# The adaLN modulation of a decoder step computed from fp32 weights as the stationary operand

## Chip, cores and metric

One NeuronCore of a Trainium2 chip. The metric is the device time of one execution in microseconds, the median of several runs. Everything (prompt group and sample group, both layers) runs in one launch on this core.

## The reference

One inference step of a decoder with two layers, for 512 prompt tokens and 8 sample tokens (one for each of 8 sequences), width 1024. A layer is three sub-layers: a SwiGLU feed-forward part (width 2816), a token mixer, another feed-forward part. That makes six sub-layers, numbered 0 to 5; 1 is the attention and retention mixer ("even"), 4 the convolution mixer ("odd"). Each sub-layer needs a shift, a scale and a gate of 1024 values for each of nine conditioning vectors (one for the prompt, eight for the samples), and it is these that the change concerns:

```python
mods = (jax.nn.silu(c) @ w_ada[l] + b_ada[l]).reshape(B, 1, N_MOD, D_MODEL)
sh, sc, g = mods[:, :, 0], mods[:, :, 1], mods[:, :, 2]
f = _swiglu(x * (1.0 + sc) + sh, w_ffn_in[l, 0], w_ffn_out[l, 0])
x = _layernorm(DEEPNORM_ALPHA * x + 0.5 * g * f, ln_g[l, 0], ln_b[l, 0])
```

`c` has 1 + 8 rows of 1024, `w_ada[l]` is 1024 x 9216 in fp32, so one sub-layer's share is 1024 x 3072, 24 column tiles of 128 (`MT`). Both groups share every weight.

## The kernel before

The activations lie turned in SBUF: 128 partitions of features, 8 tiles (`KT`), the 520 tokens in two halves of 260 (`HT`). SyncE loads the raw weights in chunks of 128 output columns (`raw`, two buffers), ScalarE makes the high part (`cut`, line 1204), POOL the low part (line 656), both two buffers deep, and TensorE multiplies (`product`). A sub-layer's first product runs over its input matrix. The second product makes 8 output tiles: in a feed-forward part two chunks of 11 tiles for each (66 matmuls a chunk), in a mixer one chunk of 8 tiles (48 matmuls). VectorE adds each output tile to the residual (`residual`) and gathers the sums for the norm; `shift_sums` and `norm_sums` (lines 802 to 819) are TensorE's part in that.

The modulation of sub-layer 0 is made at the start, from `ada_first` with the conditioning vectors stationary, plain fp32, and turned afterwards. That of sub-layers 1 to 5 is made during the second product of the sub-layer before, so in the stages of sub-layers 0 to 4, and there the change lies. Before, it goes in 24 pieces a stage. A piece is one half (4 of the 8 row tiles) of 256 columns of the weights, 512 KB, in one of `NADA` = 3 buffers (`ada_w`, line 169). Its way:

- SyncE loads it (`pieces`, line 456), once the low part of the piece three back has been cut. The table `PIECES` (line 50) says which pieces go with which chunk of the product: for a feed-forward tile 0 and 1, then 2, then 3 and 4, then 5; for a mixer three with each chunk. SyncE's queue holds chunk loads and piece loads in that order.
- ScalarE makes its high part (`high_piece`, line 1376). POOL makes the low part in feed-forward stages, VectorE in mixer stages (`low_pieces`, line 425).
- TensorE multiplies (`pieces`, lines 728 and 730): the conditioning vectors are stationary as 18 columns (9 high, 9 low, `c_parts`) with the high part of the weights moving, then as 9 columns with the low part moving, 256 columns at a time, 8 matmuls a piece. The result is 18 x 256 in PSUM.
- After two pieces ScalarE copies that to SBUF (`group_sums`, line 1381) and TensorE turns it and adds the rows of high and low (`turn_group`, line 715): two fp32 matmuls of 18 x 128 by 9 columns, into PSUM bank 6. 12 groups a stage (`GROUPS`), the last turned behind the last product.

TensorE's order is written by hand: in a feed-forward product the first piece of the chunk stands in the middle (after 30 matmuls) and a second one behind the product; in a mixer product pieces stand after 18 and 36 of the 48 matmuls and behind it. VectorE reads bank 6 in `modulation(n)` (line 1499) between the residuals and the norm.

Line 894 (`tri` or `ones`, 128 x 128 fp32, stationary, 8 columns moving) and line 912 (`kr_tok`, 128 x 128 fp32, 128 columns moving) are other fp32 matmuls of the even mixer, line 802 the sums at mid-stage.

Of the kernel before, what the change touches and what calls it, by code (L numbers as in the profile page):

```python
# [22 lines left out]
KT = D // 128  # L23
# [9 lines left out]
MT = 3 * KT  # L33
# [12 lines left out]
NADA = 3  # L46
ADA_W = 256
GROUPS = MT * 128 // ADA_W

# [20 lines left out]
def host_tables():  # L70
# [22 lines left out]
    for m in range(4):  # L93
# [6 lines left out]
    two_parts = np.zeros((128, 9), f)  # L100
    two_parts[np.arange(18), np.arange(18) % 9] = 1
    res = np.concatenate([ident, ones, ones / D, p[:, None].astype(f), gdec, tail.reshape(128, 32),
                          delta.reshape(128, 64), sel.reshape(128, 1024), bd, unit.reshape(128, 64), two_parts], axis=1)
# [20 lines left out]
def build_step(nc, a, out, last=NSUB):  # L124
# [10 lines left out]
    with ctx:  # L135
# [18 lines left out]
        def sem(name):  # L154
# [13 lines left out]
        ada_w = put("ada_w", [128, NADA, KT // 2, ADA_W], F32, R_ADA)  # L168
        ada_sums = put("ada_sums", [18, ADA_W], F32, R_ADA + NADA * 4096)

        ada_parts = {place: tuple(put(f"ada_{part}_{name}", [128, NADA, KT // 2, ADA_W], F32R, at + u * NADA * 4096)
                                  for u, part in enumerate(("hi", "lo")))
                     for place, name, at in ((False, "h", R_H), (True, "proj", R_HID))}
# [21 lines left out]
        res = new("res", [128, 1710])  # L196
# [6 lines left out]
        two_parts = res[0:18, 1701:1710]  # L203
# [4 lines left out]
        c_parts = new("c_parts", [128, KT, 18], F32R)  # L208
# [129 lines left out]
        ada_hi_cut = sem("ada_hi_cut")  # L338
        ada_cut = sem("ada_cut")
        ada_turned = sem("ada_turned")  # L340
# [78 lines left out]
        def low_pieces(eng, n, i, now):  # L419

            hi, lo = ada_parts[n == EVEN]
            for q in now:
                eng.wait_ge(ada_hi_cut, n * MT + i * 6 + q + 1)
                eng.tensor_tensor(lo[:, q % NADA], ada_w[:, q % NADA], hi[:, q % NADA].bitcast(F32),  # L425
                                  ALU.subtract).then_inc(ada_cut, 1)

# [21 lines left out]
        def _(sp):  # L449
# [1512 lines left out]
```

## Time and profile before

| | |
|---|---|
| median of 3 runs | 2734.92 us (2734.47 to 2747.84) |
| profiled execution, span from first to last instruction | 2743.9 us |
| PE busy / weight loads busy | 2498.2 us (91%) / 2240.8 us (82%) |
| VectorE / ScalarE / POOL busy | 918.1 / 846.3 / 1084.8 us |
| granted TensorE clock, mean | 0.940 |
| DMA | 298.44 MB, mean 109 GB/s |

The runs' times don't say which of them was profiled; the span is all that the profile has of its own execution, and it lies within the three runs. PE is TensorE's matmuls, PEld its weight loads, which overlap them. Each row of a timeline is a start, a length, and a line of the kernel; matmuls are pipelined, so the distance of two starts says what one occupies, not its length. The clock is a share of 2.4 GHz: 1.00 is 2.4, 0.50 is 1.2.

### The profile page before, as it was taken

How to read it: one execution, taken by the hardware profiler on the slowest of the kernel's cores; microseconds unless marked ns; L12 is line 12 of the kernel's file. 1: busy time of each engine (PE TensorE's matmuls, PEld its weight loads, DVE VectorE, ACT ScalarE, POOL GpSimd, SP SyncE). 2: the span in 40 equal slices, each digit the busy share in tenths (PEclk: the TensorE clock that was granted, in tenths of full speed). 3: DMA queues.
4: the chain of work that ended last, by engine and by line, in shares of the span. 5: the costliest groups of instructions: out<-in, count | busy, mean ns of one | idle time of the engine just before them, and what ended most of it. 6: DMA issues, size and time to landing. Idle time of an engine off the chain costs nothing.

```text
span 2743.9 us, 45520 instructions
## 1 busy us (share of the span) xinstructions
PE 2498.2 (91%) x18440; PEld 2240.8 (82%) x18440; DVE 918.1 (33%) x1069; ACT 846.3 (31%) x1176; POOL 1084.8 (40%) x544
## 2 busy tenths in 40 slices
PE   7999999799889988699999889999979886999996
PEld 2899999679742347599999889999969875999995
DVE  1122202446244445622211442220253456222214
ACT  3222333422212233332232342233333243322213
POOL 1344476424300011344466644447643323444343
PEclk9999999889969988899999989999989997999998
DMA  7233454247313334233355323335412351333321
GB/s 262 63 91 92 124 158 141 75 131 221 102 59 98 114 94 151 65 89 92 92 156 158 94 62 92 92 116 166 141 39 85 101 175 56 96 89 90 94 87 51
DMA packets 448322, 298.44 MB, mean 109 GB/s; under 512 B 20103, under 2 KB 422119, under 8 KB 448087
## 3 DMA queue, kind: packets, MB, share of 16 engines
q1 hardware_dynamic: 448214, 296.92, 36.3%
q8 instruction: 78, 1.28, 0.2%
q14 instruction: 30, 0.24, 0.0%
HBM read 291.36 MB, written 5.53 MB: 108 GB/s over the span
## 4 chain that ended last, share of the span: by engine, by line
PE 57%; DVE 7%; issue 3%; DMA 2%; ACT 2%; POOL 2%; SPq 0%; DVEq 0%; POOLq 0%; ACTq 0%
PE ps L706 45%; PE ps L975 2%; PE ps L728 1%; PE ps L730 1%; PE ps L961 1%; PE ps L965 1%; DMA raw<-w_out_odd 1%; DMA raw<-w_out_even 1%; DVE sq_sum L1588 1%; DVE ada_lo_proj L425 1%; PE ps L1014 1%; DVE ada_lo_h L425 1%; PE ps L1007 1%; DVE rdev L1626 1%; POOL w_lo L656 1%
## 5 line engine op out<-in xcount | busy, mean ns | idle before, releaser
L656 POOL TENSOR_TENSOR w_lo<-raw,w_hi 128x1024 fp32r<-128x1024 f32 (+1 forms) x308 | 802.6, 2607 | 1255.4 <-ACT w_hi L1204 1254.9
L706 PE MATMUL ps<-h_hi,w_hi 128*128 128x260 f32 x3584 | 730.0, 285 | 25.3 <-POOL w_lo L656 15.9
L706 PE MATMUL ps<-h_hi,w_lo 128*128 128x260 f32 x3584 | 728.5, 285 | 0.0
L706 PE MATMUL ps<-h_lo,w_hi 128*128 128x260 f32 x3584 | 728.3, 285 | 0.0
L1204 ACT ACTIVATE w_hi<-raw 128x1024 fp32r<-128x1024 f32 (+1 forms) x308 | 346.6, 1126 | 1233.4 <-PE ps L706 1121.3
L706 PEld LDWEIGHTS ps<-h_hi,w_hi 128*128 128x128 f32 x3584 | 560.0, 191 | 30.4 <-POOL w_lo L656 13.2
L706 PEld LDWEIGHTS ps<-h_hi,w_lo 128*128 128x128 f32 x3584 | 559.6, 191 | 0.0
L706 PEld LDWEIGHTS ps<-h_lo,w_hi 128*128 128x128 f32 x3584 | 558.7, 191 | 0.0
L706 PE MATMUL ps<-hid_hi,w_hi 128*128 128x260 f32 x1408 | 286.6, 285 | 13.8 <-DVE hid_lo L1920 13.8
L706 PE MATMUL ps<-hid_hi,w_lo 128*128 128x260 f32 x1408 | 284.9, 284 | 0.0
L706 PE MATMUL ps<-hid_lo,w_hi 128*128 128x260 f32 x1408 | 284.2, 284 | 0.0
L1917 DVE TENSOR_TENSOR gated<-silu_a,ps 128x520 f32<-128x520 f32 x88 | 61.3, 696 | 663.2 <-PE ps L706 647.2
L706 PEld LDWEIGHTS ps<-hid_hi,w_hi 128*128 128x128 f32 x1408 | 219.0, 190 | 16.7 <-DVE hid_lo L1920 14.7
L1558 DVE SCALAR_TENSOR_TENSOR x<-ps,mod,x 128x512 f32<-128x512 f32 x48 | 36.1, 751 | 567.6 <-PE ps L706 567.6
L1920 DVE TENSOR_TENSOR hid_lo<-gated,hid_hi 128x520 f32 (+1 forms) x88 | 196.9, 2238 | 81.9 <-ACT hid_hi L1475 81.9
L706 PEld LDWEIGHTS ps<-hid_lo,w_hi 128*128 128x128 f32 x1408 | 219.2, 190 | 0.0
L706 PEld LDWEIGHTS ps<-hid_hi,w_lo 128*128 128x128 f32 x1408 | 218.3, 190 | 0.0
L425 POOL TENSOR_TENSOR ada_lo_h<-ada_w,ada_hi_h 128x1024 fp32r<-128x1024 f32 x72 | 171.3, 2393 | 46.3 <-ACT ada_hi_h L1376 46.3
L746 PE MATMUL ps<-h_hi,w_hi 128*128 128x260 f32 x192 | 48.9, 341 | 85.2 <-DVE h_lo L1549 85.1
L746 PEld LDWEIGHTS ps<-h_hi,w_hi 128*128 128x128 f32 x192 | 34.5, 222 | 99.2 <-issue 88.8
L728 PE MATMUL ps<-ada_hi_h,c_parts 128*18 128x256 f32 x384 | 96.0, 284 | 12.6 <-DVE ada_lo_h L425 12.6
L1376 ACT ACTIVATE ada_hi_h<-ada_w 128x1024 fp32r<-128x1024 f32 x96 | 97.5, 1044 | 20.3 <-DMA ada_w<-w_ada 17.1
(296 smaller groups left out, 2375.8 us busy)
## 6 DMA issues: line engine op xcount, KB each, us to landing
raw<-w_ffn_in SPq DMA_DIRECT2D x176, 512.0 KB, 3.7
ada_w<-w_ada SPq DMA_DIRECT2D x120, 512.0 KB, 4.4
raw<-w_ffn_out SPq DMA_DIRECT2D x64, 704.0 KB, 4.4
pages<-cache_k SPq DMA_DIRECT2D x64, 256.0 KB, 3.0
pages<-cache_v SPq DMA_DIRECT2D x64, 256.0 KB, 3.0
raw<-w_in_even SPq DMA_DIRECT2D x28, 512.0 KB, 4.1
raw<-w_in_odd SPq DMA_DIRECT2D x24, 512.0 KB, 3.7
ada_first<-w_ada SPq DMA_DIRECT2D x5, 2048.0 KB, 14.3
```

Source lines behind the costliest of these rows:

```text
L425: eng.tensor_tensor(lo[:, q % NADA], ada_w[:, q % NADA], hi[:, q % NADA].bitcast(F32), ALU.subtract).then_inc(ada_cut, 1)
L656: pool.tensor_tensor(w_lo[:, k, 0:kt, :], raw[:, k, 0:kt, :], w_hi[:, k, 0:kt, :].bitcast(F32), ALU.subtract).then_inc(chunk_cut, 1)
L706: mm = pe.matmul(ps[:, 2 * q + half, 0:HT], w[:, k, t, :], v[:, kt0 + t, half, :], start=start and t == 0 and step == 0, stop=stop and t = ...
L728: pe.matmul(ps[0:18, 7, 0:ADA_W], c_parts[:, at, :], hi[:, q % NADA, t, :], start=at == 0, stop=False)
L730: mm = pe.matmul(ps[0:9, 7, 0:ADA_W], c_parts[:, at, 0:9], lo[:, q % NADA, t, :], start=False, stop=at == KT - 1)
L746: mm = pe.matmul(ps[:, 2 * q + half, 0:HT], w[:, k, t, :], v[:, t, half, :], start=t == 0 and step == 0, stop=t == KT - 1 and step == 2)
L975: mm = pe.matmul(ps[0:NH, 7, :], s_samp[:, b, :, g], pages[:, k, g % 4, :], start=g == 0, stop=g == NPG - 1)
L1204: act.activation(w_hi[:, k, 0:kt, :], raw[:, k, 0:kt, :], ACT.Identity).then_inc(hi_cut, 1)
L1376: act.activation(hi[:, q % NADA], ada_w[:, q % NADA], ACT.Identity).then_inc(ada_hi_cut, 1)
L1558: dve.scalar_tensor_tensor(xt[:, :, 0:HP], ps[:, 2 * q:2 * q + 2, 0:HP], g[:, 0:1], xt[:, :, 0:HP], ALU.mult, ALU.add).then_inc(drained, 1)
L1917: dve.tensor_tensor(gated[:, j], silu_a[:, j], pair(2 * j + 1), ALU.mult).then_inc(gate_done, 1)
L1920: dve.tensor_tensor(hid_lo[:, m].rearrange("p a h c -> p (a h) c"), gated[:, j], hid_hi[:, m].rearrange("p a h c -> p (a h) c").bitcast(F3 ...
```

## The change

A piece is now one column tile of 128 with all 8 row tiles, again 512 KB, as plain fp32 in one of 4 buffers. TensorE takes the weights themselves as the stationary side (128 x 128) and moves the nine conditioning vectors (`c_act`, fp32), 8 matmuls a piece, straight into the 9 columns of bank 6 that belong to the tile. There are still 24 pieces a stage at the same places. SyncE loads a piece once TensorE has used the one four back. The high and low parts of the pieces, `c_parts`, the copies, the turning, and their semaphores go. The bodies of second products on SyncE and TensorE are written out in full, 4 times. The modulation of sub-layer 0 stays.

```diff
-NADA = 3
-ADA_W = 256
-GROUPS = MT * 128 // ADA_W
+NADA = 4
...
-        ada_w = put("ada_w", [128, NADA, KT // 2, ADA_W], F32, R_ADA)
+        ada_w = put("ada_w", [128, NADA, KT, 128], F32, R_ADA)
...
-                    if not (n == 1 and is_first(i) and q < NADA):
-                        sp.wait_ge(ada_cut, c - NADA + 1)
-                    half = q % 2 * (KT // 2)
-                    sp.dma_start(ada_w[:, q % NADA, :, :],
-                                 ada_view(n)[:, half:half + KT // 2, bass.ds(i * 3 * ADA_W + q // 2 * ADA_W, ADA_W)]
-                                 ).then_inc(ada_full[q % NADA], 16)
+                    if c >= NADA:
+                        sp.wait_ge(ada_used, MT + c - NADA + 1)
+                    at = (i * 6 + q) * 128
+                    sp.dma_start(ada_w[:, c % NADA, :, :], ada_view(n)[:, :, at:at + 128]).then_inc(ada_full[c % NADA], 16)
...
-                    if q % 2 == 0 and not (is_first(i) and q == 0):
-                        turn_group(n, i * 3 + (q // 2 - 1))
-                    pe.wait_ge(ada_cut, (n - 1) * MT + i * 6 + q + 1)
-                    for t in range(KT // 2):
-                        at = q % 2 * (KT // 2) + t
-                        pe.matmul(ps[0:18, 7, 0:ADA_W], c_parts[:, at, :], hi[:, q % NADA, t, :],
-                                  start=at == 0, stop=False)
-                        mm = pe.matmul(ps[0:9, 7, 0:ADA_W], c_parts[:, at, 0:9], lo[:, q % NADA, t, :],
-                                       start=False, stop=at == KT - 1)
+                    c, tile = (n - 1) * MT + i * 6 + q, i * 6 + q
+                    if tile == 0:
+                        pe.wait_ge(mod_steps, mod_steps_before(n))
+                    pe.wait_ge(ada_full[c % NADA], c // NADA * 16 + 16)
+                    for t in range(KT):
+                        mm = pe.matmul(ps[:, 6, tile * 9:tile * 9 + 9], ada_w[:, c % NADA, t, :], c_act[:, t, :],
+                                       start=t == 0, stop=t == KT - 1)
                     mm.then_inc(ada_used, 1)
...
-                if n + 1 < last:
-                    turn_group(n + 1, GROUPS - 1)
+                for i in range(KT // 2):
+                    body(i)
...
-                        if n + 1 == last and chunk:
+                        if chunk:
                             cut(*chunk)
-                        if n + 1 < last:
-                            then = (steps + (tuple(q + 6 for q in steps[0]),))[u + 1]
-                            if static and i == KT // 2 - 1 and then[0] >= 6:
-                                then = ()
-                            modulation_parts(i, now, then, chunk)
...
-                    dve.wait_ge(ada_turned, GROUPS * n)
+                    dve.wait_ge(ada_used, MT * (n + 1))
...
-                        if n not in FFN and n + 1 < last:
-                            low_pieces(dve, n, i, PIECES[1][j])
```

## Rows read from the trace of the kernel before

**Rows 1.** the page: shares of the chain that ended last
```profile
PE 57%; DVE 7%; issue 3%; DMA 2%; ACT 2%; POOL 2%; SPq 0%; DVEq 0%; POOLq 0%; ACTq 0%
PE ps L706 45%; PE ps L975 2%; PE ps L728 1%; PE ps L730 1%; PE ps L961 1%; PE ps L965 1%; DMA raw<-w_out_odd 1%; DMA raw<-w_out_even 1%; DVE sq_sum L1588 1%; DVE ada_lo_proj L425 1%; PE ps L1014 1%; DVE ada_lo_h L425 1%; PE ps L1007 1%; DVE rdev L1626 1%; POOL w_lo L656 1%
```
**Rows 2.** stretches: busy PE, PEld, DVE, ACT, POOL; clock; sub-layers 1, 4, 0, 2, 5
```profile
1013.80:1123.50 109.70, 90.39 (x629) 81.18 (x629) 59.11 (x69) 41.40 (x53) 18.46 (x8) 0.85 0.47 144
2189.40:2293.80 104.40, 86.14 (x629) 77.91 (x629) 58.08 (x69) 40.69 (x53) 17.78 (x8) 0.90 0.51 152
336.60:496.50 159.90, 158.69 (x1297) 152.14 (x1297) 28.07 (x40) 50.98 (x59) 108.25 (x40) 0.99 0.48 139
1405.80:1564.40 158.60, 157.34 (x1297) 150.82 (x1297) 28.10 (x40) 51.00 (x59) 108.30 (x40) 1.00 0.47 140
2578.50:2708.10 129.60, 129.56 (x1060) 129.24 (x1060) 28.11 (x40) 24.27 (x22) 46.12 (x14) 0.99 0.25 73
```
**Rows 3.** who waited for whom in 1013.8 to 1123.5: total, times, longest
```profile
ACT ada_hi_proj L1376 <- DMA ada_w<-w_ada: 19.8, 8, 6.7
...
PE ps L728 <- DVE ada_lo_proj L425: 13.8, 4, 5.2
```
**Rows 4.** timeline of PE, even mixer stage: start us, us, what
```profile
1056.80 0.40 PE L706 MATMUL ps<-h_hi,w_lo 128*128 128x260 f32 x2
1057.13 0.61 PE L715 MATMUL ps<-res,ada_sums 18*128 18x9 f32 x4
1057.67 0.29 PE L728 MATMUL ps<-ada_hi_proj,c_parts 128*18 128x256 f32 x1
...
1058.61 0.40 PE L706 MATMUL ps<-h_hi,w_hi 128*128 128x260 f32 x2
```
**Rows 5.** groups of instructions, the turning
```profile
L715 PE MATMUL ps<-res,ada_sums 18*128 18x9 f32 x240 | 36.9, 259 | 14.8 <-ACT ada_sums L1381 14.8
```
**Rows 6.** timeline of PE, two runs of fp32 matmuls
```profile
747.29 0.57 PE L894 MATMUL ps<-logf,even_t 128*128 128x8 f32 x2 [2.67 <-DVE rot L1692]
...
751.13 0.57 PE L894 MATMUL ps<-logf,even_t 128*128 128x8 f32 x2
...
764.72 3.50 PE L912 MATMUL ps<-vr_tok,kr_tok 128*128 128x128 f32 x29 [3.27 <-DVE kr_tok L1717]
```
**Rows 7.** stretches, same columns, at the two runs of group 6
```profile
747.00:752.00 5.00, 4.71 (x21) 4.45 (x22) 4.59 (x7) 0.00 (x0) 0.00 (x0) 0.50 0.00 2
764.70:768.00 3.30, 3.28 (x29) 3.28 (x30) 0.00 (x0) 0.00 (x0) 0.00 (x0) 1.00 0.76 251
```
**Rows 8.** timeline of PE, a change from products to fp32 and back
```profile
425.09 0.40 PE L706 MATMUL ps<-hid_hi,w_lo 128*128 128x260 f32 x2
425.33 1.04 PE L802 MATMUL ps<-tile_sum,res 128*128 128x260 f32 x4
...
426.32 0.28 PE L730 MATMUL ps<-ada_lo_h,c_parts 128*9 128x256 f32 x1
```
**Rows 9.** timeline of PE, start of the odd mixer's second product
```profile
2189.38 0.80 PE L706 MATMUL ps<-mix_hi,w_hi 128*128 128x260 f32 x2 [0.77 <-DVE mix_lo L1890]
...
2193.34 0.28 PE L728 MATMUL ps<-ada_hi_h,c_parts 128*18 128x256 f32 x1
```
**Rows 10.** DMA issues: KB each, median us to landing
```profile
ada_w<-w_ada SPq DMA_DIRECT2D x120, 512.0 KB, 4.4
...
raw<-w_out_even SPq DMA_DIRECT2D x8, 512.0 KB, 5.7
```
**Rows 11.** the page: groups that cut a chunk of weights
```profile
L656 POOL TENSOR_TENSOR w_lo<-raw,w_hi 128x1024 fp32r<-128x1024 f32 (+1 forms) x308 | 802.6, 2607 | 1255.4 <-ACT w_hi L1204 1254.9
...
L1204 ACT ACTIVATE w_hi<-raw 128x1024 fp32r<-128x1024 f32 (+1 forms) x308 | 346.6, 1126 | 1233.4 <-PE ps L706 1121.3
```
**Rows 12.** timeline of PE, end of the even mixer's second product
```profile
1121.10 0.40 PE L706 MATMUL ps<-h_hi,w_lo 128*128 128x260 f32 x2
...
1126.12 1.14 PE L816 MATMUL ps<-sq_sum,res 128*128 128x260 f32 x4 [0.65 <-DVE sq_sum L1588]
```

More of the change, by code:

```diff
@@ L167, in build_step @@
         R_ADA = region(4 * 4096)
-        ada_w = put("ada_w", [128, NADA, KT // 2, ADA_W], F32, R_ADA)
[L169 to L174, printed above, removed]
+        ada_w = put("ada_w", [128, NADA, KT, 128], F32, R_ADA)
         R_TMP = region(5 * 4 * NTOK)
@@ L194, in build_step @@
         dev = sq[:, 0]
-        res = new("res", [128, 1710])
+        res = new("res", [128, 1701])
         ident, ones, mean_w = res[:, 0:128], res[:, 128:256], res[:, 256:384]
@@ L207, in build_step @@
         c_act = new("c_act", [128, KT, 9])
-        c_parts = new("c_parts", [128, KT, 18], F32R)
         mod = new("mod", [128, 2, MT, 9])
@@ L417, in centre_tile @@
             eng.tensor_tensor(x[:, t], x[:, t], mean[:, :, :], ALU.subtract).then_inc(centred[part], 1)
[L419 to L426, printed above, removed]
         two = lambda v: v.rearrange("p (h c) -> p h c", h=2)
@@ L590, in _ @@
                         sp.wait_ge(rows_made, 6)
-                    loop(sp, n == 0, KT // 2, body)
+                    for i in range(KT // 2):
+                        body(i)
                     continue
@@ L611, in body @@
                             pieces(n + 1, i, PIECES[1][k])
-                loop(sp, False, KT // 2, body)
+                for i in range(KT // 2):
+                    body(i)
                 if n == ODD:
@@ L679, in second_body @@
                                 cut(c, u % 2, kt)
-                                if n in FFN and n + 1 < last:
-                                    low_pieces(pool, n, i, now)
                         loop(pool, False, KT // 2, second_body)
@@ L1079, in second_product @@
             def second_product(n, body):
-                loop(pe, True, KT // 4, body)
-                body(KT // 4)
-                body(KT // 4 + 1)
-                if n + 1 < last:
-                    turn_group(n + 1, GROUPS - 1)
+                for i in range(KT // 2):
+                    body(i)
             for n in range(last):
@@ L1368, in second_product @@
                 steps = PIECES[per_tile]
-                hi = ada_parts[n == EVEN][0]
-                def high_piece(i, q):
-                    if not (is_first(i) and q < NADA):
-                        act.wait_ge(ada_used, (n + 1) * MT + i * 6 + q - NADA + 1)
-                    act.wait_ge(ada_full[q % NADA], n * MT // NADA * 16 + i * 32 + q // NADA * 16 + 16)
-                    act.activation(hi[:, q % NADA], ada_w[:, q % NADA], ACT.Identity).then_inc(ada_hi_cut, 1)
-                def group_sums(i, q):
-                    act.wait_ge(ada_used, (n + 1) * MT + i * 6 + q + 1)
-                    act.activation(ada_sums[:, :], ps[0:18, 7, 0:ADA_W], ACT.Identity).then_inc(rows_copied, 1)
-                def modulation_parts(i, now, then, chunk=None):
-                    cuts = [((now[-1] if len(now) > 1 else now[-1] + 1) - 0.5, 2, 0)] if chunk else []
-                    for _, what, q in sorted([(q, 0, q) for q in now if q % 2] + [(q - NADA, 1, q) for q in then] + cuts):
-                        if what == 2:
-                            cut(*chunk)
-                        elif what == 0:
-                            group_sums(i, q)
-                        elif q < 6:
-                            high_piece(i, q)
-                        else:
-                            high_piece(i + 1, q - 6)
                 def body(i):
@@ L1423, in second_product @@
                     act.wait_ge(ev("cat_lo"), 10)
-                if n + 1 < last:
-                    modulation_parts(0, (), steps[0])
                 loop(act, True, KT // 4, body)
@@ L1603, in residuals @@
                 for t in range(KT // 2, KT):
-                    if n not in FFN and n + 1 < last:
-                        low_pieces(dve, n, t // 2, PIECES[1][t % 2])
                     product_done(t // 2, t % 2)
```

20 lines of the change are left out of this document (1 added, 19 removed).

## The prediction, on record before the changed kernel was seen

> **What bounds the kernel now.** I read the chain that ended last first: TensorE holds 57% of it, and most of that is line 706, the products of the big weights [rows 1]. So what counts is time on TensorE in program order, and the stages in which the modulation of the next sub-layer is computed: the second products of five of the six sub-layers. The table by stretches gives them [rows 2]: the feed-forward stages 0 and 2 take 159.9 and 158.6 us (stage 3 is like stage 0), the two mixer stages (sub-layer 1, then 4) 109.7 and 104.4 us, and the last stage, which has no modulation beside its 1056 matmuls, 129.6 us. In the feed-forward stages PE is busy nearly throughout (158.7 of 159.9), so a piece of modulation costs what it occupies. In the mixer stages it is busy 90.4 of 109.7 and 86.1 of 104.4, and the granted clock is 0.85 and 0.90: there PE waits. The waits name the reason [rows 3]: PE at line 728 waits 13.8 us for the low part that VectorE cuts, and that one waits behind ScalarE's high part, which itself waits 19.8 us for the DMA of the piece (three buffers, freed late).
>
> **The change on TensorE, a piece at a time.** Before, a piece (half of the rows, 256 columns) is 8 matmuls from one start to the next product's start: 1057.67 to 1058.61, 0.94 us [rows 4]. A turn (four records) adds, from its first record's start at 1057.13, 0.54 us, and it starts late: the pair ahead began at 1056.80, its second 0.12 later, so its turn could have followed at 1057.04 and came 0.09 later. 0.63 per turn. A stage's 24 pieces and 11 turns ahead of the last product's end make 22.6 + 6.9 = 29.5 us, against the measured 159.9 - 129.6 = 30.3 [rows 2]. I take 30.3, because both stretches start at the low clock.
>
> After, a piece is 8 fp32 matmuls with 128 x 128 stationary and 9 columns moving. An fp32 matmul is two records: line 715 is called 120 times and shows x240 [rows 5]. What one record costs when little moves is the load of the stationary side. Two rows bracket it with the same 128 x 128 fp32 shape. Line 912 (128 columns moving) at clock 1.00: 29 records in 3.50 us, so 0.115 from start to start when the last one's own 0.28 is taken off, and 30 loads in 3.30 us, 0.110 each. Line 894 (8 columns moving, the nearest shape of all) at clock 0.50: from 747.29 to 751.13 lie 18 records, 0.213 each, which is 0.107 at full clock [rows 6, 7]. I take 0.112, the middle of the full clock's own: a piece is 16 x 0.112 = 1.79 us. Both ends: 16 x 0.107 = 1.71, and 1.79 + 0.18 = 1.97 if each piece also pays what the turn pays around its records (0.09 ahead and, since 0.54 - 4 x 0.112 is 0.09, as much behind). I take none of it: where a 128 x 128 fp32 load follows a product and precedes another load, the starts run through. Line 802 starts 0.24 after the start of the pair ahead, and its four records with the first matmul behind them take 0.99, which is four of 0.22 and one of 0.12 [rows 8].
>
> By the Trainium skill ("FP8 and Floating Point Precision", TensorE Precision Notes) true fp32 makes four passes through the array; with a load of columns / 1.2 ns for each pass ("TensorE: Matmul & The Clock Gate", LDWEIGHTS) a matmul would take some 427 ns as an estimate, and the 960 of them 410 us instead of 215.
>
> - Feed-forward stages, three: 24 x 1.79 = 43.0 in place of 30.3: **+12.7 each, +38**.
> - Mixer stages: 384 matmuls at 0.120 (129.6 less 0.9 for the sums at mid-stage and 1.8 for its cold start, by 1056) are 46.1, the sums 0.9, and 23 pieces ahead of the last product's end 41.2: 88.2 us if nothing waits. The start is cold: the first 18 matmuls of the odd stage last from 2189.38 to 2193.34, 3.96 instead of 2.16 [rows 9]. Then comes a piece at once, which moves little and may itself still run at 0.213 a record [rows 6] (+1.6), and the next matmuls too (+1.7). I take 4 us for the even stage and 3 for the odd. Before, from the first product's start to the last product's end: 107.7 (1013.8 to 1121.5 [rows 2, 12], 2.0 less than the stretch), and for the odd stage as much less, 102.4. So **-15.5 and -11.2, together -27**.
> - The waits that go. All three steps between DMA and PE go; PE waits for the transfer itself. It is issued when the piece four back has been used, which is some 13 us ahead (three pieces and four groups of matmuls), against 4.4 us to landing [rows 10]. The piece's own DMA has runs of 512 bytes in place of 1024, as the raw weights have: 5.7 us is their row in the even stage. SP now holds the next chunk's load behind a piece that waits for PE: in a mixer stage the chunk of product k+1 leaves once the second piece inside product k-1 is used, 14 us ahead; landing 5.7, ScalarE's cut 1.1, POOL's 2.6 [rows 10, 11] make 9.4. So nothing new is late; what comes next in the mixer stages is TensorE itself.
> - Taken from ScalarE (120 high parts, 60 copies), POOL (72 low parts) and VectorE (48 low parts): nothing in the feed-forward stages, where PE did not wait; in the mixers it is the gain above and not counted again.
> - The tail behind a stage: the sums of squares start 4.6 us after the last product's end (1121.50 to 1126.12), and what ends PE's idle time before them is VectorE's running sum [rows 12]. The last piece of a mixer stage (1.79) and the last turn both hide under it. 0. Should VectorE get 2 us faster, the piece would show.
> - The two operations that split the conditioning vector at the start: 0, they lie beside the transfers of the first modulation's weights, which PE waits for; if that cover were gone, under 1 us. Straight code in place of one loop turn on PE and SP: 0 (0 to +2).
>
> **Sum**: +38 - 27 = +11 us. Against the profiled execution: span 2743.9, after it 2755. That span is 9.0 us above the median of the runs, and I carry the difference over: 2734.9 + 11 = **2746 us**, +0.4%. Some 0.5% (13.7 us) is what a measurement of this kernel can tell from none, so this is "same", close to its edge: 2.7 us more make it slower.
>
> **Rivals.**
> *Slower, by the edges of a piece.* Each of the 120 pieces pays the 0.18 us that the turn pays when TensorE passes from the products to it and back. For it stand the turn's edges [rows 4]. Against it stands line 802 [rows 8], where the fp32 load has all 128 rows and the edge is free; the turn's has 18. Price 118 x 0.18 = +21, so 2767. It decides from 0.02 us per piece on (2.7 us by 118). Chance 0.16.
> *The clock.* A piece moves 9 columns per load, and in the mixer stages pieces are nearly half of the time. In 747 to 752 the loads were busy 4.45 of 5.00 us and the clock was granted at 0.50 throughout [rows 7], after an idle stretch; so such work at least does not bring it back. If the low level holds for a third of both mixer stages, 30 us of work in each take twice that: +60 in place of the 7 already counted, so 2799; the feed-forward stages have 3.6 us or more of dense matmuls between pieces. Against: no stretch of the trace shows a fall while PE had work in such a mix. Chance 0.09. At the low clock a record takes 0.213 [rows 6], a cold piece 3.4 us. The Trainium skill's rule for a load (columns / 1.2 ns, "TensorE: Matmul & The Clock Gate", LDWEIGHTS) names no clock and would make a cold piece 1.7 us; that row contradicts it.
> *Four loads per fp32 matmul.* A piece would be 32 x 0.112 = 3.58 us: 118 x 1.79 = +211, so 2957. Against it stand two records for each call [rows 5] and their spacing [rows 6]. Chance 0.02. It is what the four passes of the Trainium skill ("FP8 and Floating Point Precision", TensorE Precision Notes) would come to with a load for each; by the two records of the trace that rule doesn't hold for loads.
> *A transfer is late.* The chunk loads sit behind pieces on SP; if half of the mixers' wait comes back (10 us in each stage), +20 and 2766; if only the first products do, +3. Chance 0.06.
> *Faster.* The second record of a matmul is free because so little moves, or one is made: a piece is 0.9 us, 118 x 0.89 = -105, so 2641. Against: the records of 715 and 894 both came in twos at full spacing. Chance 0.04.
> *My forecast*, 0.63: own range 2737 to 2756 (piece at 1.71 to 1.83, cold starts 4 to 11 in all).
>
> **The numbers.** The range that should hold it 8 times in 10 goes from 2737 (the low end of a piece) to 2772, which takes in the edges of a piece and the late transfers, and leaves out the clock, the four loads and the halved piece (0.15) and some of the margins. Faster: 0.05 (the halved piece, and 0.01). Same: 0.45 of the forecast's 0.63 and 0.03 of the late transfer: 0.48. Slower: 0.17 of the forecast (the upper third of its range), 0.16, 0.09, 0.02 and 0.03 of the transfer: 0.47. (The last 0.01 of the forecast goes to faster.)
>
> **What would show it.** In the profile after: 1920 records of the new matmul, 0.112 from start to start at the full clock; feed-forward stages of 172 to 173 us; mixer stages of 91 to 93 to the last product's end with PE busy throughout, no wait of PE for a DMA in them, and the clock above 0.93; the sums of squares still 4.6 us behind the last product. Wrong it is if a feed-forward stage goes beyond 175 (the edges), if the clock in the mixers is under 0.8, or if PE idles there for ada_w or w_lo.

## The result, and the profile after

| | before | after |
|---|---|---|
| median of 12 runs each, same chip | 2741.93 us | 2762.06 us |
| lowest and highest of them | 2732.86, 2751.21 | 2750.59, 2794.42 |
| profiled execution: its time, span | 2747.84, 2743.9 us | 2750.59, 2748.8 us |
| granted TensorE clock of it, mean | 0.940 | 0.953 |

The ratio of after to before is 1.0082, with an interval of 1.0049 to 1.0114; it leaves out the two highest runs of after, 2793.92 and 2794.42 us, and the medians of all runs are 1.0073 apart. The last experiment shows what such a long run looks like inside. So the changed kernel is slower by 0.8%; the interval's low end, 0.49%, lies at the edge of 0.5%. The forecast was 2746 us in a range of 2737 to 2772, and a ratio of 1.004: the time lies in the range, and it is on the slower side, which had 0.47 against 0.48 for the same.

The page of after: busy times, the chain's shares, the two rows of the new matmul, and its DMA.

```profile
PE 2531.8 (92%) x19160; PEld 2318.5 (84%) x19160; DVE 860.6 (31%) x1020; ACT 710.0 (26%) x995; POOL 910.8 (33%) x472
...
PE 63%; DVE 5%; issue 2%; POOL 1%; ACT 1%; DVEq 0%; POOLq 0%; ACTq 0%
...
L693 PEld LDWEIGHTS ps<-c_act,ada_w 128*128 128x128 f32 x1920 | 225.5, 192 | 0.3
L693 PE MATMUL ps<-c_act,ada_w 128*128 128x9 f32 x1920 | 222.1, 252 | 0.0
...
ada_w<-w_ada SPq DMA_DIRECT2D x120, 512.0 KB, 3.7
```

960 matmuls are 1920 records, so two a matmul and not four. The chain leans on PE by 6% more than in [rows 1]: the new line has 6% where lines 728 and 730 had 2%, and the products 48% where they had 45%. VectorE's share fell from 7% to 5% and ScalarE's from 2% to 1%.

The stretches, to be laid beside [rows 2], with the same columns (us, busy PE, PEld, DVE, ACT, POOL, clock, DMA share, GB/s): even mixer, odd mixer, then feed-forward stages 0, 2, 3 and 5.

```profile
1017.40:1110.30 92.90, 92.87 (x780) 92.17 (x780) 28.15 (x45) 13.58 (x17) 19.10 (x8) 0.98 0.57 165
2207.00:2300.60 93.60, 93.60 (x780) 92.91 (x780) 28.17 (x45) 13.59 (x17) 19.08 (x8) 0.98 0.57 164
337.20:509.70 172.50, 172.50 (x1444) 172.17 (x1444) 28.01 (x40) 25.31 (x23) 48.19 (x15) 0.99 0.44 126
1393.20:1566.70 173.50, 173.47 (x1444) 173.15 (x1444) 28.04 (x40) 25.30 (x23) 48.23 (x15) 0.98 0.42 125
1853.00:2025.40 172.40, 172.37 (x1444) 172.08 (x1444) 28.03 (x40) 25.30 (x23) 48.21 (x15) 0.99 0.43 126
2583.50:2713.00 129.50, 129.46 (x1060) 129.14 (x1060) 28.08 (x41) 24.28 (x22) 46.11 (x14) 0.99 0.26 73
```

PE is busy in all of them to within 0.04 us: the kernel has become one whose time is TensorE's alone there. The mixer rows run some 3.5 us past the last product's end; to that end they are 89.3 and 90.1 us.

One piece in the even mixer, in the timeline of PE (start, length): 1024.95 to 1026.65.

```profile
1024.95 1.85 PE L693 MATMUL ps<-c_act,ada_w 128*128 128x9 f32 x16
1026.65 0.48 PE L680 MATMUL ps<-h_hi,w_hi 128*128 128x260 f32 x2
1026.97 0.28 PE L680 MATMUL ps<-h_lo,w_hi 128*128 128x260 f32 x1
```

The next product's start comes 1.70 us after the piece's first, and the pair behind takes 0.32 instead of the 0.24 of a pair inside a product: 1.78 us. By the single records of the trace, starts inside a piece are 0.112 apart; only the second comes 0.03 after the first, and behind the piece one start comes 0.20 instead of 0.12 after the one ahead. The two cancel, and a piece costs 16 x 0.112. The stages say the same: (172.5 - 129.5) / 24 = 1.79.

**Where the time went**, in the two profiled executions:

| part | before | after | difference |
|---|---|---|---|
| second products of sub-layers 0, 2, 3 | 159.9, 158.5, 160.0 | 172.5, 173.5, 172.4 | +40.0 |
| gap ahead of each of them | 2.86 each | 5.25 each | +7.2 |
| even and odd mixer, to the last product's end | 107.7, 102.4 | 89.3, 90.1 | -30.7 |
| sum of what the change touches | | | **+16.5** |
| attention part between the even mixer's two products | 289.9 | 282.8 | -7.1 |
| all else | | | -4.5 |

The attention row is not put down to the change: further profiles of the same changed kernel show that part at 288.8 and 289.4 us as well as at 282.8. The last row has no known cause: the change's four profiles have 1750.3 to 1753.5 us there, the one profile of before 1756.9. So the spans, 4.9 us apart, flatter the change, and the 16.5 us agree with the lowest runs (17.7 apart).

The second row of the table was in nobody's sum. A feed-forward second product starts when VectorE has made the last low part of its input (`hid_lo`). VectorE around that moment, after:

```profile
332.10 0.69 DVE L1833 TENSOR_TENSOR gated<-silu_a,ps 128x520 f32<-128x520 f32 x1 [7.60 <-PE ps L680]
333.99 3.10 DVE L1836 TENSOR_TENSOR hid_lo<-gated,hid_hi 128x520 f32 x1 [1.20 <-ACT hid_hi L1398]
```

POOL, after:

```profile
327.63 3.21 POOL L632 TENSOR_TENSOR w_lo<-raw,w_hi 128x1408 fp32r<-128x1408 f32 x1 [3.69 <-ACT w_hi L1164]
333.39 3.15 POOL L632 TENSOR_TENSOR w_lo<-raw,w_hi 128x1408 fp32r<-128x1408 f32 x1 [2.54 <-ACT w_hi L1164]
```

VectorE, before:

```profile
333.93 0.70 DVE L1917 TENSOR_TENSOR gated<-silu_a,ps 128x520 f32<-128x520 f32 x1 [7.59 <-PE ps L706]
335.83 0.70 DVE L1920 TENSOR_TENSOR hid_lo<-gated,hid_hi 128x520 f32 x1 [1.20 <-ACT hid_hi L1475]
```

POOL, before:

```profile
329.47 3.21 POOL L656 TENSOR_TENSOR w_lo<-raw,w_hi 128x1408 fp32r<-128x1408 f32 x1 [3.69 <-ACT w_hi L1204]
336.70 4.71 POOL L425 TENSOR_TENSOR ada_lo_h<-ada_w,ada_hi_h 128x1024 fp32r<-128x1024 f32 x2 [4.02 <-ACT ada_hi_h L1376]
```

The same operation takes 0.70 us alone and 3.10 us beside POOL's cut, 2.4 us more, on the path. Before, POOL's next work was the low part of a piece, and that waited for ScalarE until `hid_lo` was done; with those gone, POOL goes straight to the cut of the second chunk. The Trainium skill states such a contention ("GPSIMD Engine Reference", Specifications): GpSimd shares its SBUF interfaces with VectorE and contends with its instructions that have two SBUF inputs, as `hid_lo` has. The trace agrees with it.

The price could be read in the trace of before. There the median of the 88 `hid_lo` is 2.29 us; only the last one ahead of a second product is on the path. Stage 5, which has no pieces, had the gap of 5.25 us already. VectorE and POOL ahead of it, before:

```profile
2575.36 3.09 DVE L1920 TENSOR_TENSOR hid_lo<-gated,hid_hi 128x520 f32 x1 [1.20 <-ACT hid_hi L1475]
...
2574.74 3.15 POOL L656 TENSOR_TENSOR w_lo<-raw,w_hi 128x1408 fp32r<-128x1408 f32 x1 [2.54 <-ACT w_hi L1204]
```

### The profile page after: what moved, and what is told of

The parts are those of the page before. It is cut to its first block, busy times and chain, and to the rows that moved or that the text cites. A ratio compares the mean times of both kernels' runs of the same rounds, so it can differ in the third digit from the quotient of the medians.

```text
span 2748.8 us, 45846 instructions
## 1 busy us (share of the span) xinstructions
PE 2531.8 (92%) x19160; PEld 2318.5 (84%) x19160; DVE 860.6 (31%) x1020; ACT 710.0 (26%) x995; POOL 910.8 (33%) x472
## 4 chain that ended last, share of the span: by engine, by line
PE 63%; DVE 5%; issue 2%; POOL 1%; ACT 1%; DVEq 0%; POOLq 0%; ACTq 0%
PE ps L680 48%; PE ps L693 6%; PE ps L938 2%; PE ps L924 1%; PE ps L928 1%; PE ps L977 1%; PE ps L970 1%; DVE rdev L1545 1%; DVE x L1468 1%; POOL samp_t L415 0%; PE ps L709 0%; POOL w_lo L632 0%; DVE sq_sum L1511 0%; PE ps L948 0%; PE ps L998 0%
## 5 line engine op out<-in xcount | busy, mean ns | idle before, releaser
L680 PEld LDWEIGHTS ps<-h_hi,w_hi 128*128 128x128 f32 x3584 | 556.4, 190 | 31.3 <-POOL w_lo L632 15.1
L680 PE MATMUL ps<-hid_hi,w_hi 128*128 128x260 f32 x1408 | 294.2, 290 | 21.0 <-DVE hid_lo L1836 21.0
L1836 DVE TENSOR_TENSOR hid_lo<-gated,hid_hi 128x520 f32 (+1 forms) x88 | 204.0, 2318 | 81.9 <-ACT hid_hi L1398 81.9
L693 PEld LDWEIGHTS ps<-c_act,ada_w 128*128 128x128 f32 x1920 | 225.5, 192 | 0.3
L693 PE MATMUL ps<-c_act,ada_w 128*128 128x9 f32 x1920 | 222.1, 252 | 0.0
L709 PE MATMUL ps<-h_hi,w_hi 128*128 128x260 f32 x192 | 47.0, 329 | 88.2 <-DVE h_lo L1472 88.0
L709 PEld LDWEIGHTS ps<-h_hi,w_hi 128*128 128x128 f32 x192 | 32.2, 207 | 103.5 <-issue 84.8
```

Of the source, the lines that this page charges most:

```text
L680: mm = pe.matmul(ps[:, 2 * q + half, 0:HT], w[:, k, t, :], v[:, kt0 + t, half, :], start=start and t == 0 and step == 0, stop=stop and t = ...
L693: mm = pe.matmul(ps[:, 6, tile * 9:tile * 9 + 9], ada_w[:, c % NADA, t, :], c_act[:, t, :], start=t == 0, stop=t == KT - 1)
L709: mm = pe.matmul(ps[:, 2 * q + half, 0:HT], w[:, k, t, :], v[:, t, half, :], start=t == 0 and step == 0, stop=t == KT - 1 and step == 2)
L1836: dve.tensor_tensor(hid_lo[:, m].rearrange("p a h c -> p (a h) c"), gated[:, j], hid_hi[:, m].rearrange("p a h c -> p (a h) c").bitcast(F3 ...
```

## The experiments

Times are medians; a ratio is to the kernel before, run on the same chip in turn. "Tail" is the time from a mixer's last product's end to the next first product.

**again, again2, again3: the changed kernel itself.**

> The changed kernel itself, for a second trace and the spread of its runs. Its 12 runs went from 2750.6 to 2794.4 us with a mean granted clock of 0.953 down to 0.937; the profiled one was the fastest. Theory A (the pieces move so little that the granted clock now and then falls in the stretches that hold them): a run above 2765 shows the clock lower in the second products of the mixers or the feed-forward parts. Theory B (the spread is the older one, in the even mixer's attention and at the norms, where the pieces play no part): a slow run shows its extra low-clock time outside the stretches with pieces, which stay at 172.5 and 90 us.

> The changed kernel once more, to catch a slow execution in a trace. If it is above 2765, the clock theory says that a mixer stage is over 100 us long at a clock under 0.9, and all feed-forward second products within 2 us of 172.5; the rival says that the extra lies outside both mixer stages.

> As again2: a slow execution (above 2765) has a mixer stage over 100 us by the clock theory; by the rival its extra time lies outside the mixer stages.

again: 2756.14 us (2750.32 to 2783.0, 8 runs), ratio 1.0061 (1.0034 to 1.0089); its profile has a span of 2752.9 us, the profiles of again2 and again3 have 2760.3 and 2748.1 us. Feed-forward stages 172.4 to 173.5 in all three, odd mixer 89.5 to 90.1, gaps 5.2 to 5.3. What moves is the even mixer: 90.3 us at clock 0.973, 93.5 at 0.936, 89.3 at 0.984, and the attention part ahead of it (288.8, 289.4, 282.8). The size of the piece is settled; the spread upward is not, for none of these profiles is of a run over 2765 us. But again2 shows its mild form in the change itself: the even mixer from its start to where the clock rises, well past the first piece, and from there to its end.

```profile
1026.50:1038.30 11.80, 11.80 (x55) 11.80 (x56) 0.00 (x0) 0.00 (x0) 0.00 (x0) 0.50 0.15 44
1038.50:1119.90 81.40, 81.40 (x704) 81.28 (x703) 24.72 (x40) 11.88 (x15) 16.69 (x7) 1.00 0.63 182
```

**hold: POOL waits for the last low part.** The change, and this on POOL:

```diff
+                                if n in FFN and is_first(i) and u == 1:
+                                    pool.wait_ge(hid_lo_done, FT * ffns_before(n) + FT)
...
-                        loop(pool, False, KT // 2, second_body)
+                        loop(pool, True, KT // 2, second_body)
```

> POOL waits, in each feed-forward second product, with the low part of the second chunk until VectorE's last low part of the hidden layer is done. Theory 1 (the 3.1 instead of 0.7 us of that last VectorE operation, with POOL cutting beside it, is what lengthened the wait ahead of each feed-forward second product from 2.8 to 5.3 us): the operation is back at 0.7, the gap at 2.8, in four stages, and the kernel is 8 to 11 us faster than the changed one (about 2741 at its fastest). Theory 2 (the gap is due to something else, such as a later load of the first chunk): the gap stays 5.3 and the time within 2 us of the changed kernel's.

The gaps went to 2.9 us in all four feed-forward stages; VectorE's low part, in the timeline of hold:

```profile
335.35 0.70 DVE L1838 TENSOR_TENSOR hid_lo<-gated,hid_hi 128x520 f32 x1 [1.20 <-ACT hid_hi L1400]
```

Stage 5 became 127.9 us at clock 1.00. The shorter gap allows that and doesn't ensure it: with gaps of 2.9 us hold2 and late have 130.5 and 129.4 us there, and with a gap of 5.25 us no feed-forward stage of any trace has the clock at 1.00 throughout. The mechanism of the gap is right. The median is not: 2772.89 us (2752.51 to 2783.59, 5 runs), ratio 1.0129 (1.0106 to 1.0152), worse than the change without the wait. The profile happened to be of the fastest run, and even that has 93.5 us at clock 0.936 in the even mixer. So it compares best with again2, which has the same 93.5: the spans are 2750.4 and 2760.3 us, 9.9 apart, and four gaps shorter by 2.4 us come to 9.6.

**spread: the piece's matmuls dealt out singly.** One or two of them ahead of each feed-forward tile from the fourth on, three ahead of each mixer tile from the second on and behind the last, in place of eight together.

```diff
-                                        between=lambda t: pieces(n + 1, i, now[:1]) if t == FH // 2 else None)
+                                        between=lambda t: pieces(n + 1, i, now, ((t - 3) * len(now), (t - 2) * len(now))) if t >= 3 else None)
-                                pieces(n + 1, i, now[1:])
...
-                                    between=lambda t: pieces(n + 1, i, now[t // 3 - 1:t // 3]) if t in (3, 6) else None)
+                                    between=lambda t: pieces(n + 1, i, now, ((t - 1) * 3, t * 3)) if t >= 1 else None)
```

> The same fp32 matmuls, but no longer 8 in a row: one or two of them ahead of each of 8 tiles of a feed-forward chunk, three ahead of each tile of a mixer's. If passing between products and fp32 loads costs nothing (my prediction's choice), the stages stay at 172.5 and 90 us within 1; if an edge costs 0.1 us or more, each feed-forward stage grows by over 10 us. If the spread of the runs up to 2794 comes from stretches of 1.8 us that move little, the slowest run comes down to within 20 us of the fastest; if not, it stays some 40 us wide.

2880.86 us (2874.7 to 2903.39, 6 runs), ratio 1.0523 (1.0491 to 1.0554). The feed-forward stages took 172.4, 172.6 and 171.9 us, with 128 changes from products to fp32 matmuls in a stage in place of 24: an edge costs nothing. Both mixers became far longer instead; their stretches in spread:

```profile
1019.00:1185.00 166.00, 165.89 (x768) 165.51 (x768) 25.39 (x41) 12.34 (x15) 17.11 (x7) 0.50 0.32 92
2283.60:2420.70 137.10, 137.09 (x769) 136.77 (x769) 24.72 (x40) 11.89 (x15) 16.54 (x7) 0.62 0.39 112
```

The even mixer runs at 1.2 GHz from its first matmul to its last, 166 us, with PE busy for 165.9 of them and its loads for 165.5. The clock was low at the start, as before and after, and in this mix it did not rise. The two stages cost 166.0 + 137.1 - 179.4 = +124 us, which is the experiment's excess.

**hybrid: the change in the mixers alone**, the feed-forward stages as before (24 pieces of 256 columns, high and low parts, turned), three buffers for both.

```diff
+                    if n - 1 not in FFN:
+                        at = (i * 6 + q) * 128
+                        sp.dma_start(ada_w32[:, q % NADA, :, :], ada_view(n)[:, :, at:at + 128]).then_inc(ada_full[q % NADA], 16)
+                        continue
...
-                for q in pieces_now:
+                for q in pieces_now if n - 1 not in FFN else ():
+                    c, tile = (n - 1) * MT + i * 6 + q, i * 6 + q
...
+                for q in pieces_now if n - 1 in FFN else ():
```

> The kernel before in the three feed-forward stages (high and low parts, moving, turned), the change in the two mixer stages alone. By the stages' own lengths: mixers 90 instead of 108 and 102 us, feed-forward stages 160 and their gaps 2.8 as before, so 30 us faster than before (ratio about 0.989), and some 45 faster than the changed kernel. If the gain in the mixers were the lottery of the clock and not the waits that went, it would be under 10 us.

2716.84 us (2712.54 to 2747.01, 12 runs), ratio 0.9925 (0.9901 to 0.9949): faster than both kernels, by less than the 0.989 expected. Its two mixers and a feed-forward stage:

```profile
1011.80:1124.60 112.80, 112.79 (x759) 112.68 (x759) 22.90 (x38) 11.25 (x14) 16.61 (x7) 0.76 0.48 136
2191.60:2281.20 89.60, 89.60 (x759) 89.48 (x759) 21.92 (x38) 11.25 (x14) 15.80 (x7) 0.98 0.60 172
334.00:493.90 159.90, 157.50 (x1287) 151.11 (x1288) 28.77 (x41) 52.18 (x60) 108.22 (x40) 0.99 0.48 141
```

One run holds both outcomes: the odd mixer takes 89.6 us at clock 0.98, the even one, with the same matmuls and PE as busy, 112.8 at 0.76.

**late: no piece until the mixer's first product is through.** hold, and in each mixer no piece inside the first product, one behind it, four in the second, three in each later one and two behind the last. The loads on SyncE move with them: the last seven pieces stand ahead of the next sub-layer's first chunk.

```diff
+MIX_AT = ({8: (0,)}, {2: (1,), 4: (2,), 6: (3,), 8: (4,)}, *({3: (3 * k - 1,), 6: (3 * k,), 8: (3 * k + 1,)} for k in range(2, 7)),
+          {3: (20,), 6: (21,), 8: (22, 23)})
...
-                                    between=lambda t: pieces(n + 1, i, now[t // 3 - 1:t // 3]) if t in (3, 6) else None)
+                                    between=lambda t: pieces(n + 1, 0, at.get(t, ())))
```

> The changed kernel with POOL's wait of the run hold, and in the two mixer stages the 24 pieces moved back: none inside the first product, one behind it, four in the second, three in each of the next ones, two behind the last. So a mixer stage begins with 48 dense matmuls. Clock theory (the mixer stages start at the low clock, and a piece after 18 matmuls can keep them there; that is where the spread of 2750 to 2794 comes from): the even stage is 90 to 92 us in every trace, its clock above 0.93, the slowest run lies within 15 us of the fastest, and the median comes down to some 2745. Rival (the spread comes from elsewhere, such as the attention part ahead of it): the spread stays 30 us and the median near 2760.

2741.8 us (2734.12 to 2749.95, 12 runs), ratio 1.0006 (0.9991 to 1.002). The highest of twelve runs is below the lowest of the change's 20 timed runs, 2750.32. Mixers 88.3 and 88.4 us, the tails 24.7 in place of 21.7. By the trace the longer tail begins with a transfer. SyncE's issue of the next sub-layer's first chunk in late, and in late2 below, whose even mixers end at 1110.28 and 1115.00:

```profile
1101.65 10.08 SPq L433 DMA_DIRECT2D raw<-w_ffn_in  x3
...
1103.16 8.75 SPq L433 DMA_DIRECT2D raw<-w_ffn_in  x3
```

Three waits of late follow from it:

```profile
ACT w_hi L1169 <- DMA raw<-w_ffn_in: 12.9, 1, 12.9
DVE sq_sum L1516 <- ACT sq L1131: 6.3, 1, 6.3
PE ps L784 <- DVE sq_sum L1516: 0.6, 1, 0.6
```

The chunk is asked for 8.6 us ahead of the last product's end in place of 11.8, since it stands behind pieces that wait for PE. ScalarE waits for it with the squares for VectorE's running sum behind it, and PE's sums of squares start 7.3 us after the last product's end in place of 4.6.

**late_nohold: late without POOL's wait.**

> This is the kernel 'late' (no piece inside a mixer's first product, one behind it, four in the second, three in each later product, two behind the last) without the wait that keeps POOL's cut of the second chunk behind VectorE's last low parts. Theory (that wait is worth the difference of the gaps ahead of a feed-forward stage's second product, 5.2 or 5.3 against 2.8 us, in four stages): the gaps are 5.2 to 5.3 us again, and the time is about 10 us over late: a median near 2751 us, a ratio to the kernel before of 1.003 to 1.005. Rival (the wait is worth nothing or costs, as the median of 'hold' by itself suggested, 2772.9 against 2756 and 2762 of the change): a median of 2742 us or less, ratio 1.000 or below.

2755.7 us (2742.32 to 2757.97, 8 runs), ratio 1.0045 (1.0027 to 1.0063). Gaps 5.2 or 5.3 us again. Against late the wait is worth 1.0045 - 1.0006 = 0.0039, some 10.7 us for four stages; the rival falls. Its highest of eight runs is 2758: without the wait too, the late places show no long run. Its tails are 23.1 and 22.0 us, with the same two pieces behind the last product. The sums of squares start 5.8 and 7.6 us after that product there, so a tail's length hangs on more than their start: in the shorter one three of VectorE's steps for the modulation took 0.23 us each where late has 1.2 to 1.3.

**late2: one piece behind the last product**, four in the third, and six pieces' loads ahead of the next chunk in place of seven.

```diff
-MIX_AT = ({8: (0,)}, {2: (1,), 4: (2,), 6: (3,), 8: (4,)}, *({3: (3 * k - 1,), 6: (3 * k,), 8: (3 * k + 1,)} for k in range(2, 7)),
-          {3: (20,), 6: (21,), 8: (22, 23)})
+MIX_AT = ({8: (0,)}, {2: (1,), 4: (2,), 6: (3,), 8: (4,)}, {2: (5,), 4: (6,), 6: (7,), 8: (8,)},
+          *({3: (3 * k,), 6: (3 * k + 1,), 8: (3 * k + 2,)} for k in range(3, 8)))
```

> As late, with one piece instead of two behind a mixer's last product and four instead of three in its third. Theory (the longer stretch from a mixer's last product to the next stage's first one, 24.7 us against 21.7, comes from the second piece behind the last product, which the norm's sums wait for): the two stretches are back at 21.7 to 22 us, the stages of the products are longer by one piece, 1.8 us, and the sum is 1 to 3 us under late for each mixer: a median near 2738 us, ratio 0.998 to 1.000. Rival (the stretch is longer because the clock is low at its beginning or for another reason): it stays at 24 us or more, and the median is above late's 2742 us.

2740.43 us (2737.08 to 2752.16, 12 runs), ratio 1.0008 (0.9993 to 1.0022). The tails are 21.8 and 21.8, as expected, but not for the reason given: by late's trace PE, done with both pieces, still waited for VectorE ahead of the sums. What also came back is the lead of the next chunk's load, 11.8 us, and with it the sums' start, 4.6 us. The mixers became 90.6 and 89.5. By parts that is 2.4 us less (5.8 in the tails, back 3.4 in the mixers); in the ratios nothing of it can be told.

**best and best2: hybrid with the places of late and of late2**, and POOL's wait in stage 5.

> The run hybrid (kernel before in the feed-forward stages, the change in the mixers) with the pieces moved back in the mixers as in the run late, three buffers, and POOL's wait in the last feed-forward part alone. By the stages' lengths 30 + 2 us faster than before: ratio 0.986 to 0.990, fastest run near 2705, and a spread under 15 us where hybrid had 34. If the clock in the mixers isn't what spread hybrid's runs, its median stays at 2717.

> As best (the feed-forward stages as before the change, the mixers with the fp32 pieces placed late, POOL's wait in the last feed-forward stage), with one piece instead of two behind a mixer's last product and four in the third. Theory: as for late2, 1 to 3 us a mixer under best: a median near 2709 us, ratio 0.988 to 0.990. Rival: the median is at or above best's 2713.3 us.

best: 2713.33 us (2709.37 to 2715.45, 5 runs), ratio 0.9908 (0.9892 to 0.9923). best2: 2711.59 us (2707.0 to 2715.16, 5 runs), ratio 0.9895 (0.9878 to 0.9911). These are the fastest kernels of the study, and the runs of each lie within 8.2 us where hybrid's twelve span 34.5.

**hold2: hold again.**

> The kernel 'hold' once more, unchanged: the wait for VectorE's last low parts ahead of POOL's cut of the second chunk, with the mixers' pieces where the change puts them. By itself it came out at 2772.9 us, a ratio of 1.0129, against 1.0061 and 1.0082 for the change without it, although its trace showed three gaps shorter by 2.4 us; beside the mixers' dense first product the same wait brought 14 us (2741.8 against 2755.7). Theory (the wait works alike in both, and the median of 'hold' was drawn high by the mixers, whose first product meets a piece while the clock is low, so that runs of one kernel lie far apart): the runs spread again from about 2745 to above 2780, and the ratio comes out somewhere between 1.002 and 1.013, its trace with gaps of 2.8 us. Rival (with the wait the even mixer starts in a worse phase of the clock, every time): a ratio of 1.010 or more again, an even mixer of 93 us or more.

2780.77 us (2751.55 to 2788.29, 6 runs), ratio 1.012 (1.0079 to 1.0161). Both expectations hold by their own numbers, so the run doesn't decide between them. But this time the profile is of a long run, span 2780.9 us. Its gaps are 2.9 us, its feed-forward stages 172.2, 170.8, 170.8, and its odd mixer is 90.0. The even mixer, from its start to where the clock rises, and from there to its end:

```profile
1026.80:1100.00 73.20, 73.20 (x340) 73.20 (x341) 4.80 (x12) 3.17 (x3) 7.12 (x3) 0.50 0.33 94
1102.00:1149.10 47.10, 47.10 (x406) 46.98 (x406) 19.96 (x28) 8.72 (x12) 9.55 (x4) 1.00 0.62 177
```

It took 122.3 us, 33.0 more than the 89.3 of after in that execution, with over 73 us of it at half speed. PE was busy for all of it. The first records of that stage in hold2 (the first pair, the last pair ahead of the first piece, the piece, the next pair):

```profile
1026.79 0.80 PE L682 MATMUL ps<-h_hi,w_hi 128*128 128x260 f32 x2 [8.89 <-DVE h_lo L1767]
...
1030.42 0.64 PE L682 MATMUL ps<-h_hi,w_lo 128*128 128x260 f32 x2
1030.86 3.42 PE L695 MATMUL ps<-c_act,ada_w 128*128 128x9 f32 x16
1034.12 0.78 PE L682 MATMUL ps<-h_hi,w_hi 128*128 128x260 f32 x2
```

The same stage in late: its first pair, the pair in which the clock rises, the first pair at full speed, and the first piece.

```profile
1022.03 0.80 PE L685 MATMUL ps<-h_hi,w_hi 128*128 128x260 f32 x2 [8.89 <-DVE h_lo L1770]
...
1026.09 0.58 PE L685 MATMUL ps<-h_hi,w_hi 128*128 128x260 f32 x2
1026.51 0.40 PE L685 MATMUL ps<-h_lo,w_hi 128*128 128x260 f32 x2
...
1029.88 1.85 PE L698 MATMUL ps<-c_act,ada_w 128*128 128x9 f32 x16
```

And the first stretches of it in after, where the clock rose early:

```profile
1017.40:1019.40 2.00, 1.97 (x9) 1.97 (x10) 0.00 (x0) 0.00 (x0) 0.00 (x0) 0.50 0.00 0
1019.40:1021.40 2.00, 2.00 (x16) 2.00 (x15) 0.00 (x0) 0.00 (x0) 0.00 (x0) 0.75 0.00 0
1021.40:1023.40 2.00, 2.00 (x20) 2.00 (x20) 0.00 (x0) 0.00 (x0) 0.00 (x0) 1.00 0.00 0
```

Each starts at the low clock behind 8.9 us of idle PE. In after it rose some 3 us in, still inside the 18 product matmuls ahead of the first piece; in late 4.1 to 4.5 us in, inside the 48. In hold2 the 18 were through at 4.07 us, the piece came, and the clock stayed low until 74 us into the stage. By the clock's records of every trace, it rose in the even mixer 3.0 us (after), 4.9 (again), 11.9 (again2), 2.8 (again3), 12.0 (hold), 74 (hold2) and 54 us (hybrid) after the stage's start where pieces stand in the first product, and in spread not within the stage; with a dense first product it rose after 4.3 to 5.7 us in all five (late, late_nohold, late2, best, best2). So a dense first product is what carries the stage over; without it the stage depends on when the clock happens to rise. Of the 42 timed runs of these five kernels none lies more than 15.9 us above the lowest of its kernel; of the 43 runs with the change's pieces in the first product (the change's 20, hold's eleven, hybrid's twelve), 18 lie more than 17 us above it.

## Why the prediction was right or wrong

**The cost of a piece: right.** The whole sum hung on 0.112 us for one fp32 record of 128 x 128 with little moving, taken between [rows 6] and [rows 7]: a piece of 1.79 us. Measured: 1.79. Three feed-forward stages: +38 foretold, +40.0 found. The surplus of 2.0 is stage 2 (173.5 us at clock 0.98, where 1.00 stood in [rows 2]). The clock was at 1.00 throughout in six of the 24 such stages with the short gap (all traces of before, hybrid, best, best2, hold, hold2, late and late2) and in none of the 18 with the long one, so the surplus goes with the missed step below; how much of it is chance, one profile of each kernel doesn't tell.

**The edges rival: fell.** spread made 128 edges of 24 and the feed-forward stages did not grow. Four loads a matmul and a halved piece fell with the 1920 records at 0.112 us from start to start. The Trainium skill's four passes for fp32 ("FP8 and Floating Point Precision", TensorE Precision Notes) show in no count of loads here; what they do inside a record no run shows.

**The mixers: mechanism right, size a little under.** -15.5 and -11.2 were foretold, -18.4 and -12.3 found in the profiled execution. PE is busy throughout, no DMA wait of PE is left in the even mixer, and SP's queue with the pieces ahead of the chunks delayed nothing in the changed kernel (in late it did). The term that was mis-sized is the cold start: 4 and 3 us assumed, 89.3 - 88.2 = 1.1 and 90.1 - 88.2 = 1.9 found, when the clock rises early; in again2 it is 93.5 - 88.2 = 5.3 for the even mixer, and in hold2 34.

**"Taken from ScalarE, POOL and VectorE: nothing in the feed-forward stages": this step failed.** It asked whether PE waited inside those stages, and not what the removed work had kept apart at their start. POOL's low part of a piece had held it back from VectorE's last `hid_lo`; without it POOL's cut runs beside it, 0.70 us become 3.10, and PE waits for just that. Price 3 x 2.4 = 7.2 us, and up to 2 of clock. hold shows the mechanism in its gaps and late against late_nohold its worth, 10.7 us with stage 5's own gap included.

**The tail: right.** After, the sums of squares start at 1111.39 with the last product's end at 1106.76: 4.6 us, as in [rows 12]. It is VectorE's running sum that ends the wait, as foretold. late shows what the cover hangs on: there that sum came later, behind ScalarE and a chunk that was asked for 3.2 us later, and the start moved to 7.3 us.

**The clock rival, 0.09: right as a mechanism, and in a good part of the runs.** "No stretch of the trace shows a fall while PE had work in such a mix" was true and beside the point: it need not fall, it fails to rise, since a mixer stage starts low. It was priced at a third of both mixers low (2799 us); hold2 shows one mixer low for 73 us, +33. Of the change's own 20 timed runs six lie between 2773 and 2795 us, which is where such a stage puts them; of the change itself only the mild form is in a trace (again2, 93.5 us). Their mean clocks, 0.937 to 0.944 against 0.948 to 0.953 for the other 14, say that the extra is time at the low clock: the run with a span of 2792.6 us lost (1 - 0.937) x 2792.6 = 176 us to it, the profiled one (1 - 0.953) x 2748.8 = 129, so 47 more, and its span is 44 longer. That it is lost in a mixer stage rests on hold2 and hybrid, and on late's absence of such runs.

**The base.** The forecast stood on the three runs of before shown, 2734.9; twelve gave 2741.9. Of the 16 us between 2746 and 2762, 7.0 are that. In the ratio, 1.0082 against 1.004, the rest stands: 0.0042 by 2742 are 11.5 us, against the failed step's 7 to 9 and what the clock adds to a median, which lies a few us above the early-rise runs.

**The range: held in part by luck.** The forecast's own range ended at 2756. The wider one reached to 2772 for two rivals that both fell, the edges of a piece and a late transfer; what filled it was a gap that no sum had, the clock, whose rival the range left out, and the low base.

**Open.** Why hold's runs were long more often (nine of eleven above 2770 us) than the change's (six of 20). hold2's rival, a worse phase of the clock with the wait, is not excluded. Its stage starts later, at 1026.8 and 1026.9 against 1016.9 to 1026.5 of the change, but hold, started at 1026.9, came out at 93.5 us as again2 did, and hold2 at 122.3. No run separates this.

## What to carry to other kernels

When a change takes work from an engine that is not the bound, ask what that work had kept apart: here a wait on POOL had shielded a VectorE operation on the path, and one semaphore wait brings the shield back. An fp32 product with the weights stationary costs two loads a matmul, 1.79 us a piece with 9 columns moving: it loses against moving the weights in fp32r (30.3 / 24 = 1.26 us a piece) where TensorE is full, and wins where the cutting of high and low parts is what TensorE waits for. So it was worth taking in the mixers only: best2 has 0.9895, late2, with the same places and the change everywhere, 1.0008. A transfer that stands behind others in a queue can be late for a reader two engines away: move pieces, and look where the next stage's first chunk leaves. And after an idle stretch give TensorE its dense matmuls first and the loads with little to move later; look at several runs' spread, for one profile may show only the lucky ones.

## What was not expected of the hardware

- The clock stayed at 1.2 GHz for 166 us in spread and 73 us in hold2 while PE and its loads were busy without a break, in a mix of product matmuls (260 columns moving) and fp32 ones (9 columns). The Trainium skill ("TensorE: Matmul & The Clock Gate", What's actually happening) has the gate follow how busy TensorE has been; by the busy rows alone these stretches would run at full speed, and they did not.
- At 1.00 the same mix does not pull the clock down: the rest of a mixer stays at it once the clock has risen (81.4 us in again2, 47.1 in hold2). Low and high are both held by the same work.
- A VectorE subtraction of two SBUF operands, 128 x 520, took 3.10 us beside a POOL operation of 3.15 us in place of 0.70: it ended 0.55 us after POOL's.
- Changing between fp32r and fp32 matmuls of 128 x 128 costs nothing measurable: 172.4, 172.6 and 171.9 us with 128 changes a stage, 172.5, 173.5 and 172.4 with 24.
